# Two of six modulation rows made before the token mixer, the other four inside its first three steps

## What is computed

```python
mod = jax.nn.silu(c) @ w_ada + b_ada              # (1024) @ (1024, 6144)
sh1, sc1, g1, sh2, sc2, g2 = jnp.split(mod, 6, -1)
h = x * (1 + sc1) + sh1
proj = h @ w_in                                   # q, k, v, a, g
...
mix = jnp.concatenate([attn, conv], -1) @ w_out
x = layer_norm(ALPHA * x + (1 + g1) * mix, ln1_g, ln1_b)
h2 = x * (1 + sc2) + sh2
ff = hier_moe(h2, ...)
x = layer_norm(ALPHA * x + (1 + g2) * ff, ln2_g, ln2_b)
```

## Time and profile before

| | us |
|---|---|
| three timed runs | 1628.01, 1636.15, 1651.61 |
| median of them | 1636.15 |
| the profiled execution | 1632.99 |
| its span, first to last instruction | 1631.2 |
| busy in the span: PE, DVE, ACT, POOL | 1398.7, 1300.8, 795.6, 533.2 |
| mean granted clock of PE, of full speed | 0.938 |

### The profile page before, as it was taken

The page is one execution under the profiler, slowest core; times in us unless marked ns, Lnnn a source line. Parts: engine busy times, 40 slices in busy tenths (PEclk is TensorE's granted clock), DMA queues, the critical chain, the costliest instruction groups (busy, mean ns, idle before and its releaser), DMA issues. The chain is left out here.

```text
span 1631.2 us, 25759 instructions
## 1 busy us (share of the span) xinstructions
PE 1398.7 (86%) x7082; PEld 774.3 (47%) x7082; DVE 1300.8 (80%) x3336; ACT 795.6 (49%) x1443; POOL 533.2 (33%) x388
## 2 busy tenths in 40 slices
PE   5987899999999999999997643899999999997565
PEld 1113555666656666666665322444444454443221
DVE  0521999989989898989999126899989999995588
ACT  0411344444344434444443200788888888885122
POOL 0002024455544344445544430122222222220653
PEclk9998899999999999999997665899999999998798
DMA  9955002111110111111111128557996322232897
GB/s 323 399 218 170 16 1 79 53 53 52 52 51 28 39 52 39 52 52 52 39 43 41 39 87 287 185 201 266 333 346 256 117 104 103 104 114 99 233 331 245
DMA packets 90720, 218.28 MB, mean 134 GB/s; under 512 B 8034, under 2 KB 42758, under 8 KB 88591
## 3 DMA queue, kind: packets, MB, share of 16 engines
q1 hardware_dynamic: 65554, 136.25, 23.3%
q0 software_dynamic: 11808, 43.00, 8.8%
q10 hardware_dynamic: 13277, 38.20, 6.0%
HBM read 165.90 MB, written 51.56 MB: 133 GB/s over the span
## 5 line engine op out<-in xcount | busy, mean ns | idle before, releaser
L969 DVE SCALAR_TENSOR_TENSOR y_sum<-uT,w_dw_cols,y_sum 128x128 f32<-128x128 f32 (+1 forms) x1972 | 511.2, 344 | 0.0
L1690 DVE SCALAR_TENSOR_TENSOR w_gate_up_lo<-w_gate_up_ring,w_gate_up_hi 128x2048 f16<-128x2048 f16 x96 | 219.4, 2287 | 35.0 <-ACT w_gate_up_hi L1612 35.0
L1612 ACT ACTIVATE w_gate_up_hi<-w_gate_up_ring 128x2048 f16 x96 | 182.8, 1907 | 60.4 <-SPq L1570 39.5
L1096 PE MATMUL bank<-w_in_hi,hT_hi 128*128 128x512 f16 (+3 forms) x544 | 193.9, 356 | 1.1 <-DVE hT_lo L1078 1.1
L1096 PE MATMUL bank<-w_in_lo,hT_hi 128*128 128x512 f16 (+3 forms) x544 | 193.6, 356 | 0.0
L1096 PE MATMUL bank<-w_in_hi,hT_lo 128*128 128x512 f16 (+3 forms) x544 | 193.2, 355 | 0.0
L1593 POOL COPY slot_index<-slot_token 128x1 int32 (+1 forms) x48 | 57.0, 1188 | 350.1 <-PE eturn L1754 307.5
L1733 PE MATMUL ps_up<-w_gate_up_hi,slot_rowsT_hi 128*128 128x512 f16 x384 | 147.2, 383 | 21.8 <-DVE slot_rowsT_lo L1715 21.8
L1733 PE MATMUL ps_up<-w_gate_up_lo,slot_rowsT_hi 128*128 128x512 f16 x384 | 146.8, 382 | 0.0
L1733 PE MATMUL ps_up<-w_gate_up_hi,slot_rowsT_lo 128*128 128x512 f16 x384 | 146.7, 382 | 0.0
L727 POOL TENSOR_TENSOR y_small<-y_small,mhalf 128x1 f32<-128x1 f32 (+1 forms) x17 | 9.3, 549 | 364.3 <-DVE y_small L1000 364.3
(11 more groups left out here) (256 smaller groups left out, 2935.9 us busy)
## 6 DMA issues: line engine op xcount, KB each, us to landing
w_ada_ring<-in_w_ada SPq DMA_DIRECT2D x12, 2048.0 KB, 14.7
expert_rows<-out_rows ACTq DMA_DIRECT2D x48, 512.0 KB, 2.7
w_gate_up_ring<-in_w_gate SPq DMA_DIRECT2D x16, 1024.0 KB, 8.7
w_gate_up_ring<-in_w_up SPq DMA_DIRECT2D x16, 1024.0 KB, 12.0
w_down_ring<-in_w_down SPq DMA_DIRECT2D x16, 1024.0 KB, 12.9
x_h<-in_x_prompt SPq DMA_DIRECT2D x16, 512.0 KB
x_res<-in_x_prompt SPq DMA_DIRECT2D x16, 512.0 KB, 3.3
hidden<-h SPq DMA_DIRECT2D x16, 512.0 KB, 2.6
```

Source lines behind the costliest of these rows:

```text
L969: dve.scalar_tensor_tensor(total, u, w, y_sum[:, c, :n], ALU.mult, ALU.add).then_inc(taps_done, 1)
L1096: mm = pe.matmul(out, x[xp][:, k, :n], w[wp][:, k, cols], start=(k == 0 and wp == xp), stop=(k == KD - 1 and xp == 1))
L1612: act.activation(gate_up_parts[0][:, at, k:k + KD // 2, :, :].rearrange("p k a n -> p (k a n)"), w_gate_up[:, bass.ds(b, 1), k:k + KD // 2 ...
L1690: dve.scalar_tensor_tensor(flat[1], w_gate_up[:, bass.ds(b, 1), k, :, :].rearrange("p b k a n -> p (b k a n)"), W_SCALE, flat[0], ALU.mult ...
```

## The change

The setup computes only rows 0 and 1 (sh1 and sc1), in eight products of 256 columns (line 436 of the changed kernel). `c_silu` is first copied to 128 columns, 64 for the sample and 64 for the prompt (`c_tiled`, in the memory of `x_res`), so that a product lands on all partitions as a row: partitions 0 to 63 hold the sample's, 64 to 127 the prompt's. VectorE adds the bias row, which was loaded broadcast (line 466), and does one `lo` after each. GpSimd modulates the sample tile in the setup, and `mix` begins with it in place.

The 16 products of the four other rows are done in `mix`, two at each of eight places: in step 0 after the projection kv ("scores") and at the end ("turned"); in steps 1 and 2 at these two and after the projection a ("router"). They are written into the two `score` banks (line 1218) and emptied by VectorE (lines 1030 to 1052), which waits for them where they stand in its order; TensorE waits until the bank is emptied before the scores that follow. SyncE loads 16 blocks of 1 MB for them into a ring of two (line 664), each as soon as VectorE has used the product that held the block before.

```diff
-ADA_CHUNKS = 12
-ADA_COLS = 6 * D // ADA_CHUNKS
+ADA_COLS = 256
+ADA_QUARTERS = D // ADA_COLS
+ADA_FIRST = 2 * ADA_QUARTERS
+ADA_LATER = [(v, q) for v in (2, 3, 4, 5) for q in range(ADA_QUARTERS)]
+ADA_SLOTS = {"scores": {0: 0, 1: 2, 2: 5}, "router": {1: 3, 2: 6}, "turned": {0: 1, 1: 4, 2: 7}}
...
+                for h in range(2):
+                    load_ada(h)
+                for v in range(2):
+                    sp.dma_start(M["rows"][:, 1 - v, :], a["b_ada"][:, v * D:(v + 1) * D].to_broadcast([P, D])).then_inc(b_rows_loaded, 16)
+                sp.dma_start(M["x_h"][:SMP, 0, :], a["x_sample"]).then_inc(x0_loaded, 16)
+                for h in range(2, ADA_FIRST):
+                    load_ada(h)
...
+                pool.wait_ge(x0_loaded, 16)
+                pool.wait_ge(mod_ready, ADA_FIRST)
+                pool.tensor_tensor(M["x_h"][:SMP, 0, :], M["x_h"][:SMP, 0, :], M["rows"][:SMP, 0, :], ALU.mult).then_inc(x0_ready, 1)
...
+                pe.wait_ge(c_ready, 4)
+                for h in range(ADA_FIRST):
+                    pe.wait_ge(ada_loaded[h % ADA_RING], 16 * (h // ADA_RING + 1))
+                    if h >= 2:
+                        pe.wait_ge(mod_ready, h - 1)
                     for k in range(KD):
-                        mm = pe.matmul(ps_mod[c % 2][:], c_silu[:, k:16:KD], w_ada[:, c % ADA_RING, k, :], start=(k == 0), stop=(k == KD - 1))
+                        mm = pe.matmul(ps_mod[h % 2][:, 0:ADA_COLS], c_tiled[:, k, :], w_ada[h % ADA_RING][:, k, :], start=(k == 0), stop=(k == KD - 1))
                     mm.then_inc(ada_done, 1)
...
+                for h in range(ADA_FIRST):
+                    v, q = divmod(h, ADA_QUARTERS)
+                    dve.wait_ge(ada_done, h + 1)
+                    part = M["rows"][:, 1 - v, q * ADA_COLS:(q + 1) * ADA_COLS]
+                    dve.scalar_tensor_tensor(part, ps_mod[h % 2][:, 0:ADA_COLS], 1.0 * v, part, ALU.add, ALU.add).then_inc(mod_ready, 1)
+                    rest(h)
+                for i in range(ADA_FIRST, len(pieces)):
+                    rest(i)
...
-                load_x((0, 0))
-                for v in range(2):
-                    sp.dma_start(rows[:, v, :], row(v, 1)).then_inc(in_rows_loaded, 16)
-                sp.dma_start(rows[:, 2, :], row(2, 1)).then_inc(gate_row_loaded, 16)
-                for v in range(3, 5):
-                    sp.dma_start(rows[:, v, :], row(v, 1)).then_inc(rows_loaded, 16)
+                def load_ada(h):
+                    if h >= 2:
+                        sp.wait_ge(ada_used, h - 1)
+                    sp.dma_start(w_ada[h % 2], ada_v[:, :, ada_columns(*ADA_LATER[h])]).then_inc(ada_loaded[h % 2], 16)
...
+                    if is_tile(i, 1):
+                        sp.wait_ge(gate_row_ready, 1)
+                        sp.dma_start(vec_rows[2, 0:1, :], rows[SMP:SMP + 1, 2, :]).then_inc(mod_stored, 16)
+                        for h in range(6, 12):
+                            load_ada(h)
+                        load_last(0)
...
+                def use_ada(h):
+                    v, q = ADA_LATER[h]
+                    cols, acc = slice(q * ADA_COLS, (q + 1) * ADA_COLS), score[h % 2][:, 0, :]
+                    dve.wait_ge(ada_done, h + 1)
...
+                    elif v == 4:
+                        dve.scalar_tensor_tensor(rows[:, 3, cols], acc, 1.0, rows[:, 3, cols], ALU.add, ALU.add).then_inc(shifted, 1)
+                        dve.wait_ge(shifted, 3 * q + 1)
+                        dve.tensor_tensor(acc, rows[:, 3, cols], ln1_rows[:, 1, cols], ALU.mult).then_inc(shifted, 1)
+                        dve.wait_ge(shifted, 3 * q + 2)
+                        dve.wait_ge(ada_used, h - ADA_QUARTERS + 1)
+                        dve.tensor_tensor(rows[:, 3, cols], rows[:, 3, cols], ln1_rows[:, 0, cols], ALU.mult).then_inc(shifted, 1)
+                        dve.tensor_tensor(rows[:, 4, cols], acc, rows[:, 4, cols], ALU.add).then_inc(ada_used, 1)
...
+                def ada_product(h):
+                    pe.wait_ge(ada_loaded[h % 2], 16 * (h // 2 + 1))
+                    if h >= 2:
+                        pe.wait_ge(ada_used, h - 1)
+                    for k in range(KD):
+                        mm = pe.matmul(score[h % 2][:, 0, :], c_tiled[:, k, :], w_ada[h % 2][:, k, :], start=(k == 0), stop=(k == KD - 1))
+                    mm.then_inc(ada_done, 1)
...
                     if j0 is not None:
                         project(j0, "kv", slice(K0, K0 + 2 * KVW))
+                    ada_slot(i, "scores")
                     if j1 is not None:
+                        ada_emptied(i, "scores")
                         score_round(j1, 2)
                         score_round(j1, 3)
```

More of the change, by code:

```diff
@@ L180, in build @@
             }
+            M["x_h"] = held("x_h", [P, 2, D])
+            M["rows"] = held("rows", [P, 5, D])
+            M["x_res"] = held("x_res", [P, D])
+            M["late"] = held("late", [P, 4, D])
             setup(nc, a, K, M, vec_rows, bias_rows)
@@ L527, in mix @@
         u_out = sb("u_out", [P, CH])
-        v1 = sb("v1", [P, D])
-        n1 = sb("n1", [P, D])
-        h2 = sb("h2", [P, D])
-        h2T = sb("h2T", [P, KD, P])
+        v1, n1, h2 = (M["late"][:, n, :] for n in range(3))
+        h2T = M["late"][:, 3, :].rearrange("p (k t) -> p k t", k=KD)
+        w_ada, c_tiled, ada_v = ada_ring(M), ada_silu(M), ada_view(a)
         nmax = sb("nmax", [P, HEADS])
@@ L800, in step @@
                             act.wait_ge(out_done, count(2, j, h + 1))
+                            if h == 0 and is_tile(j, 0):
+                                act.wait_ge(ada_used, len(ADA_LATER))
                             if h == 0 and not is_tile(j, 0):
@@ L971, in step, with use_slot @@
+                def use_slot(i, place):
+                    if isinstance(i[0], int) and i[1] in ADA_SLOTS[place]:
+                        for h in range(2):
+                            use_ada(2 * ADA_SLOTS[place][i[1]] + h)
                 def step(i):
```

208 lines of the change are left out of this document (124 added, 84 removed).

## The result

The changed kernel takes **1673.22 us** (median of four runs, 1671.29 to 1674.62) against 1636.35 on the same chip; the ratio is **1.0227**, 95% interval 1.0182 to 1.0271. The interval reaches to both sides of 2%: that the change makes the kernel slower is clear, that it does so by more than 2% is not. The forecast was 1648, and the measured time lies 3 us above the end of its range. The profiled execution took 1671.29 us with a span of 1669.5, so against the span before (1631.2) 38.3 us were added.

The account below looks back on a forecast made before the run. The prediction took TensorE to bound the mixer's first steps and transfers to bound the setup ahead of its last chain. It summed 1633 - 45.6 (setup) + 61 (mixer) = 1648 us, range 1612 to 1670.

Parts of the forecast that it names:

- What bounds the kernel: Mixer steps 0 to 3: TensorE has almost no free time, 7.45 us in the first three, so added work there is paid.
- The setup's term: Setup: the sample tile's first turn comes at 86.5 instead of 132.1 us, 45.6 us gained, bounds 30 to 60.
- The first product at 20.0: Setup: c_silu ready at 18.7, two copies of 0.68 us each, then TensorE's first product starts at 20.0 us.
- The first `hi` begins at 38: Setup: first hi at 38 instead of 42 us; earlier small turns, and 2 us off flipped_bias's load and store.
- Four more at 3.7 end at 63: Setup: after product 3, four more products at 3.7 us each end at 63 us, about when the pieces would.
- The mixer's term: Mixer steps 0 to 2: the 16 products add 59.2 - 4 + 6 = 61 us, bounds 52 to 76.
- − 4 + 6: Mixer steps 0 to 2: 4 us of TensorE's free time filled by products, 6 us of new waits for VectorE added.
- Costed at nothing: Mixer: VectorE's some 10 us of adds, ScalarE's and GpSimd's waits on ada_used, and the 16 block transfers cost 0.
- (a): Mixer: products hide in TensorE slack; steps 1 and 2 cost VectorE's 10 us, step 0 its 15; 1612 us, chance 0.10.
- (b): Setup keeps its pitch because the ring of three sets it; tile turned at 102, 1664 us, chance 0.10.
- (c): Mixer: products run at the lower clock, 7.4 us each; nine of 12 in steps 1 and 2 give 1681, chance 0.08.
- (d): Mixer: the products' weight loads are not hidden, 16 x 3.2 = 51 us more, 1699 us, chance 0.04.

Follow-up runs that it names:

- e1: Changed kernel, but each of the 16 mixer products makes only the first of its 8 k; 1632.08 us, ratio 0.9991.
- e3: Changed kernel, but in the setup VectorE makes nsink behind the two copies of c_silu; 1664.20 us, one run.
- e11: Changed kernel with nsink behind the c_silu copies, a setup ring of four, and step 2's y statistics ahead of the first taps; 1663.05 us, ratio 1.0176.
- e7: Changed kernel, but GpSimd modulates the sample tile only after VectorE's last lo; 1669.71 us, one run.
- e5: Changed kernel with pairs of products moved up one place, so none stands at "turned" of step 1; 1671.57 us, ratio 1.0232.
- e10: Changed kernel, but in step 2 VectorE takes y's statistics and two rounds of scores ahead of its first taps; 1671.32 us, ratio 1.0201.
- e6: Changed kernel with all 24 products in the setup, four banks, nsink behind the copies; the mixer keeps only the ln1 merge; 1639.71 us, ratio 1.0037.
- e8: As e6, but blocks of half the k and 512 columns (2 KB rows), and the merge at the start of step 0; 1624.27 us, ratio 0.9918.
- e4: Changed kernel, but the setup's ring of w_ada blocks has four places instead of three; 1661.89 us, one run.
- e2: Changed kernel, but in step 2 TensorE repeats the k and v projection twice ahead of its wait for y_tok; 1668.92 us, ratio 1.0196.

## Why the prediction was wrong, point by point

**What bounds the kernel: right.** TensorE had no room in the first steps, and the products were paid there (e1). The first number of the sum, "16 products of 3.7 us are 59.2 us", measured 59.7. That it fits so closely is luck in part: six pairs took 3.6 us a product, and two pairs at the lower clock made up for it.

**The setup's term, wrong in size: 45.6 forecast, 34.7 measured**, inside its bounds (30 to 60). By its own way points the first `hi` was 4.7 us late (42.72 for 38), the last piece of `w_in` 12.3 (77.34 for 65), the last piece of all 13.6 (96.15 for 82.5), and the turn 10.9, since it came 1.24 us behind that piece and not 4. Three steps failed. "The first product at 20.0": the copies stand behind `nsink`, which waits for the small loads until 21.36, a wait that could be read from the code; it was 22.25. "The first `hi` begins at 38": 42.72, for the load of `flipped_bias`, issued at 32.8 (29.3 in e3, without that wait), took 8.1 us and not less than the 6.3 of the earlier trace rows. "Four more at 3.7 end at 63": the last block was waited for 4.93 us, the product after it took 5.91 instead of 3.72, and it ended at 74.94. Mending the first and the last gives back 8.1 of the 10.9 us missing (e11); the rest is open. "GpSimd modulates long before, beside the pieces" was a fourth fault, but one that cost at most 1.5 us at the end (e7).

**The mixer's term, wrong in size: 61 forecast, 70.2 measured.** The products were right, and so were steps 0 and 1 (40.27 and 56.22 against "near 40 and 55"). The step that failed is "− 4 + 6", which was + 10.5, and nearly all of it lies in step 2 (77.45 against 66): TensorE's free time in the three steps was not filled by 4 us but grew from 7.45 to 15.8. (The three marks 40, 55 and 66 are 57 us above the kernel before, not the 61 of the sum.) The sentence behind it was that the waits in TensorE's free time "move along with the work: the turn of `y_tok` waits 1.75 us". That 1.75 was no constant. Before, TensorE came to this turn through work at half clock, and VectorE had begun its taps 2 us ahead of the step's first score (192.39):

```profile
190.35 1.35 DVE L964 TENSOR_SCALAR y_sum<-uT,w_dw_cols,cols 128x128 f32<-128x128 f32 x4
...
200.90 0.68 DVE L995 BATCH_NORM_STATS2 y_stat<-turn 64x6 f32<-64x512 f32 x1
```

Now TensorE comes to it at full clock after 6.4 us instead of 9.6, and VectorE, held by the additions of the pair at the border (without that pair, in e5, it begins 4.0 us ahead of the step), begins its taps with the step and ends them 10.4 us behind the first score instead of 8.5: 3.2 + 1.9 = 5.1 us of wait more, which is the difference of 6.83 and 1.75. Only the 1.9 lengthen the step, as the turn of `y_tok` comes 13.28 us behind the first score instead of 11.37.

That is not yet step 2's excess, which is 34.0 us less three pairs of 7.07, so 12.8 us. The rows of the kernel before that belong to the two later waits:

```profile
206.88 1.16 PE L1117 MATMUL score<-kT,qT 64*128 64x128 f32 x8
...
222.44 0.66 PE L1089 MATMUL turn<-ident,gate 128*128 128x128 f32 x4
```

It waited at neither. So the waits for VectorE add 1.9 + 1.78 + 2.47 = 6.2 us, and the remaining 6.6 fall to work at the lower clock, the pair of 8.61 us among it. The waits are the same in the four other kernels with this mixer, but step 2 takes only 74.21 to 74.39 us there, 3.1 to 3.2 less, with a higher clock: the mixer's term is 67.2 to 67.7 in them, and the 70.2 of the changed kernel's profile is a high one. With the statistics first the wait before `y_tok` goes, and 2.4 to 6.5 us of step 2 with it (e10, e11).

**Costed at nothing.** No product in the mixer waited for a block: right. VectorE's additions were to be free "since it waits for TensorE anyway"; at the border of step 2 they were not. That no later step would make anything good was nearly right: step 3 gave back 1.3 us. But every second step behind it became some 0.8 us longer (4.1 us in all), with TensorE waiting 0.79 to 1.07 us before the turn of `y_tok`, where the kernel before shows no such wait; the kernels with products in the mixer have these longer steps (some 47.2 against 46.4 us), e6 and e8 have not. Why is open: it was not tried.

**The rivals.** (a), that the products hide, is excluded by e1. (b) lies at 102 for the first turn, and 97.39 lies nearer to it than to the forecast's 86.5; the ring of three was indeed a part (e4). (c), the clock, was the right direction with the wrong place: only two of the eight pairs were slow (8.15 and 8.61 instead of 7.07 us), not nine products of twelve; what ran at 1.2 GHz was the other work behind the waits. (d), that weight loads are not hidden, is excluded: a product of 16 loads of 128 columns in float32 took 3.5 us, and in step 1 weight loads were busy for 38.27 us while TensorE worked for 54.06 of 56.22. The rule weighed in the prediction, from the Trainium skill, "TensorE: Matmul & The Clock Gate", Part 3 (What overlaps and what doesn't), does not hold for these rows; the measurement decides.

**The range** went to 1670. "With the bounds of its terms the case spans 1626 to 1668" does not follow: −60 with 52 gives 1625, −30 with 76 gives 1679. The range should have held the joint case that came: a setup near its upper bound and a mixer above its middle, each inside its own bounds.

## What to carry to other kernels

Moving work out of a stage pays only if the stage that takes it has room on the engine that does it: here 59.7 us of products bought 34.7 us of setup, while with all 24 products in the setup, beside the transfers (e8), the first turn still came 5.5 us sooner than in the kernel before and the mixer kept its length. A wait read from a trace is a difference of two arrival times; before it is carried over into a forecast, ask what clock each engine came with and whether the change moves either. And when one edit gives a gain, try its neighbours alone before adding their gains: two edits of the setup gave 5.2 and 5.3 us alone, and 6.7 to 8.1 together.

## What the runs showed of the hardware that was not expected

**Rows of 1 KB move more slowly than rows of 2 KB.** With the queues' share above 1.0 the setup of e6 moved 371 GB/s, that of e8 394, and the kernel before 395; the bytes of a block and the order of the loads were the same in e6 and e8. So it is in the two stretches of 20 us ahead as well, 370 and 353 GB/s in e6, 376 and 404 in e8.

**VectorE and GpSimd slow each other.** Two `lo` of 1.23 us took 3.37 and 3.36 us beside two instructions of GpSimd of 2.33 us, which took 3.96 and 3.21 (e7 has them apart). The Trainium skill, "SBUF — State Buffer", SBUF: two separate sides, says that the two share one pair of ports, which one of them holds for a whole instruction while the other waits, where VectorE's instruction has two inputs in SBUF (as a `lo` has) and GpSimd's reads SBUF. The trace agrees, for they end in turn, each about its own time behind the other: the `lo` of `w_in` at 77.34, GpSimd at 79.54, a `lo` at 80.62, GpSimd at 82.82, a `lo` at 83.90.

**More work can take less time.** In e2 48 matmuls were added to a wait and the stretch behind it became 1.4 to 3.0 us shorter, with the clock at 1.00 (2.4 GHz) where it was 0.50. The whole step gained 0.5 to 3.7 us.

**The clock also falls in the steady loop, now and then.** In e1, e10 and e11 one step of the loop, and in e6 two, were 4.4 us longer than their neighbours; in the ten other profiles none was. Each time it is the same place in a step, among the products of `pT` in attention, 0.3 to 0.5 us behind a wait of 0.31 us, and the clock stays at 0.50 for 10.2 us. By stretches of 4 us (of e10):

```profile
335.00:339.00 4.00, 3.69 (x32) 3.43 (x30) 4.00 (x16) 1.07 (x2) 3.52 (x2) 0.95 0.40 133
339.00:343.00 4.00, 4.00 (x22) 4.00 (x21) 4.00 (x16) 0.59 (x1) 0.00 (x0) 0.50 0.02 4
```

TensorE had been free for no more than 0.31 us of the stretch ahead; the same instructions run at 1.00 in the other steps. What releases it stays open. A total from a single profile thus carries an uncertainty of some 4 us a time, which only marks inside the trace, or repeated runs, take out.
